# Dividing softmax probabilities inside the turning matmul, and one table set for Exp and Ln

## The reference, cut to what matters

```python
# first block: window attention (with a sink logit in the denominator)
p = jax.nn.softmax(logits, axis=-1);  o = einsum(p_win, v_i) + einsum(p_ctx, v_ctx)
# second block, NSA: three branches, each with its own gate
p = jnp.where(mask, jnp.exp(s - m), 0.0);  p = p / jnp.maximum(jnp.sum(p, -1), 1e-30)
o = gb[..., 0:1] * o_c + gb[..., 1:2] * o_s + gb[..., 2:3] * o_w
# second block, stick-breaking, 8 heads
log_rem = jnp.where(mask, jax.nn.log_sigmoid(-z), 0.0)
suffix = lax.cumsum(log_rem, axis=3, reverse=True) - log_rem
a = jnp.where(mask, jnp.exp(jax.nn.log_sigmoid(z) + suffix), 0.0)
# second block, memory cross attention, 4 heads
p = jax.nn.softmax(s, axis=-1)
```

## Time and profile before

| | us |
|---|---|
| median of 3 runs | 2379.2 (2374.57 to 2381.82) |
| the profiled execution | 2376.95 |
| its span | 2374.9 |
| TensorE busy | 2217.8 (93%) |
| VectorE busy | 1099.2 (46%) |
| ScalarE busy | 774.9 (33%) |

### The profile page before, as it was taken

How to read it: one execution, slowest core, us unless ns; L and a number is a source line. 1 busy time by engine, 2 the same in 40 slices (tenths; PEclk the granted TensorE clock), 3 DMA queues, 4 the chain that set the end, 5 groups by cost and what they waited for, 6 DMA issues and landing times.

```text
span 2374.9 us, 25076 instructions
## 1 busy us (share of the span) xinstructions
PE 2217.8 (93%) x10572; PEld 1763.5 (74%) x10572; DVE 1099.2 (46%) x1550; ACT 774.9 (33%) x1149; POOL 87.5 (4%) x84
## 2 busy tenths in 40 slices
PE   6997889999994999999999999899988898999999
PEld 4665678888873888888888888777755576888887
DVE  3637755555528433333534333453474346443421
ACT  4314432222223322222322222323455735222211
POOL 0000000000001000000111100100000001111100
PEclk9999999999996999999999999899887998999999
DMA  7521146555530232323223223223100021323232
GB/s 261 188 88 59 58 133 197 184 195 167 192 103 18 90 106 89 102 98 96 93 92 98 95 98 100 68 90 114 39 1 1 0 72 36 107 89 106 85 98 84
DMA packets 190784, 236.59 MB, mean 100 GB/s; under 512 B 4096, under 2 KB 175392, under 8 KB 190544
## 3 DMA queue, kind: packets, MB, share of 16 engines
q1 hardware_dynamic: 189696, 230.42, 30.1%
q0 software_dynamic: 976, 4.57, 0.6%
HBM read 231.96 MB, written 2.10 MB: 99 GB/s over the span
## 4 chain that ended last, share of the span: by engine, by line
PE 83%; DVE 8%; ACT 6%; issue 2%; DMA 0%; POOL 0%; SPq 0%; DVEq 0%; ACTq 0%; POOLq 0%
PE ps L402 24%; PE ps L403 24%; PE ps L404 24%; ACT pr L611 2%; PE ps L998 1%; PE ps L848 1%; PE ps L468 1%; PE ps L649 1%; DVE pr L636 1%; PE ps L1979 1%; PE ps L582 1%; PE ps L684 1%; DVE wl L351 1%; PE ps L381 1%; DVE sa L1397 1%
## 5 line engine op out<-in xcount | busy, mean ns | idle before, releaser
L402 PE MATMUL ps<-xh,wh 128*128 128x512 f32 x1800 | 714.8, 397 | 48.5 <-DVE xl L694 26.5
L403 PE MATMUL ps<-xl,wh 128*128 128x512 f32 x1800 | 708.1, 393 | 0.0
L404 PE MATMUL ps<-xh,wl 128*128 128x512 f32 x1800 | 707.3, 393 | 0.0
L351 DVE TENSOR_TENSOR wl<-raw,wh 128x2048 fp32r<-128x2048 f32 (+1 forms) x170 | 379.0, 2230 | 493.8 <-ACT wh L339 493.8
L402 PEld LDWEIGHTS ps<-xh,wh 128*128 128x128 f32 x1800 | 341.9, 190 | 128.6 <-issue 25.8
L339 ACT CAST wh<-raw 128x2048 fp32r<-128x2048 f32 (+1 forms) x170 | 314.5, 1850 | 340.7 <-PE ps L404 263.1
L404 PEld LDWEIGHTS ps<-xh,wl 128*128 128x128 f32 x1800 | 341.7, 190 | 73.1
L403 PEld LDWEIGHTS ps<-xl,wh 128*128 128x128 f32 x1800 | 342.1, 190 | 72.0 <-issue 1.2
L402 PE MATMUL ps<-hh,wh 128*128 128x512 f32 x704 | 274.1, 389 | 0.0
L404 PE MATMUL ps<-hh,wl 128*128 128x512 f32 x704 | 273.9, 389 | 0.0
L403 PE MATMUL ps<-hl,wh 128*128 128x512 f32 x704 | 273.9, 389 | 0.0
(11 more groups left out here) (331 smaller groups left out, 1892.4 us busy)
## 6 DMA issues: line engine op xcount, KB each, us to landing
raw<-in_ffn_w SPq DMA_DIRECT2D x52, 1024.0 KB, 5.4
raw<-in_ada_w SPq DMA_DIRECT2D x42, 1024.0 KB, 5.2
raw<-in_ffn_wg SPq DMA_DIRECT2D x22, 1024.0 KB, 5.4
raw<-in_ffn_wu SPq DMA_DIRECT2D x22, 1024.0 KB, 5.3
raw<-in_ffn_w SPq DMA_DIRECT2D x16, 896.0 KB, 4.6
raw<-in_ffn_wd SPq DMA_DIRECT2D x16, 896.0 KB, 4.7
raw<-in_w_in SPq DMA_DIRECT2D x10, 1024.0 KB, 5.2
raw<-in_ffn_wd SPq DMA_DIRECT2D x8, 1024.0 KB, 5.0
```

Source lines behind the costliest of these rows:

```text
L351: e.tensor_tensor(wl[s][:, 0:n], r[:, 0:n], wh[s][:, 0:n].bitcast(F32), ALU.subtract).then_inc(*WLO.up(i))
L402: e.matmul(dst, ah, bh, start=start, stop=False)
L403: e.matmul(dst, ah, bl, start=False, stop=False)
L404: return e.matmul(dst, al, bh, start=False, stop=stop)
```

## The change

`dve_scale` no longer writes the probabilities. It writes, for each head of the job, a 128x128 diagonal matrix that holds the reciprocals, into `tmp[job parity]`, with one tensor_tensor of the identity (repeated over heads) and the column (repeated over the row). `pe_turn` waits once for it, and uses an ordinary f32 matmul of the undivided probabilities by that diagonal in the place of the transpose by the identity. In the loop of ScalarE, ahead of the first stick-breaking head, a set of tables is loaded by name that holds both Exp and Ln.

```diff
-            for g in range(nh):
-                p = prs[J.name][:, J.par, g, 0:J.width]
-                e.tensor_scalar(p, p, rs[:, g:g + 1], None, ALU.mult).then_inc(*VS.up((J.name, "scaled", J.n, g)))
+            eye = ident.unsqueeze(1).broadcast_to([P, nh, P])
+            e.tensor_tensor(diagonal(J), eye, rs.unsqueeze(2).broadcast_to([P, nh, P]), ALU.mult).then_inc(
+                *VS.up((J.name, "diagonal", J.n)))
+
+        def diagonal(J):
+
+            return tmp[J.par][:, 0:J.heads * P].rearrange("p (g q) -> p g q", q=P)
 
         def pe_turn(e, J, banks=(4, 5, 7)):
-            first = True
+
+            e.wait_ge(*VS[J.name, "diagonal", J.n])
...
                     for g in range(J.heads):
-                        if first:
-                            e.wait_ge(*VS[J.name, "scaled", J.n, g])
                         o = (b * J.heads + g) * P
-                        m = e.transpose(bank[0:w, o:o + P], prs[J.name][:, J.par, g, col:col + w], ident)
-                    first = False
+                        m = e.matmul(bank[0:w, o:o + P], prs[J.name][:, J.par, g, col:col + w], diagonal(J)[:, g],
+                                     start=True, stop=True, skip_group_check=True)
...
                 elif s < NN + 8:
+                    if s == NN:
+                        e.preload_act_table_set("natural_log_exp_and_others")
                     act_stick_logs(e, s - NN)
```

## The result

The changed kernel takes 2355.9 us (median of 4 runs, 2353.6 to 2360.0) against 2379.9 (4 runs of before, 2374.6 to 2381.8). The ratio is 0.9909, with a 95% interval of 0.989 to 0.9928. So it is 24 us faster by the medians, and 23.3 us by the two profiled executions (2376.95 and 2353.65).

What follows compares the result with a forecast made beforehand. Chains round three engines, TensorE close behind, bound the attention stages. First attention -1.5, NSA -1, stick-breaking -11, clock -5, memory 0 make -18.5 from 2376.95: 2358.5, given as 2360 since the median is 2.25 higher; own range 2354 to 2366, outer 2345 to 2374.

Steps and rivals of the forecast that it cites:

- Table loads: Stick-breaking heads: 16 loads become one ahead of them; -11 us including 1.7 for longer turning; 1.24 us gained a steady head.
- The larger figure for a table switch: Stick-breaking heads: the Trainium skill's about 2.66 us a switch, drain included, 42.6 us in all; set aside for 1.28 a load.
- Turning and dividing: Three attentions: VectorE's shorter division is paid back by longer TensorE turns; first attention -1.5 us, NSA -1, memory 0.
- The clock: Stick-breaking stage: half of the 10 us lost at the low clock comes back as TensorE's waits shorten, -5 us.
- rival A: NSA and stick-breaking: every slow stretch goes as TensorE works almost without pause; -31.5 us, 2348; chance 0.14.
- B: Rival: only the loads pay, slow stretches stay or move; -10.5 us, 2369; chance 0.15.
- C: Rival: longer turning is exposed in narrow NSA jobs and at 1.2 GHz; about +10.5 us, 2390; chance 0.08.
- D: Rival: loads are still placed between Exp and Ln in the stick-breaking heads; 2378, no change; chance 0.05.

Runs made afterwards that it cites:

- the two kernels with fewer sums: Changed kernel and kernel before, each without the three matmuls a head that add the sums of later blocks: 2346.6 and 2380.3 us, one execution each.
- the tables alone: Kernel before with only the named table set added, transposes and divisions as before: 2361.2 us, ratio 0.993.
- the one with matmuls: Kernel before with the named table set, and turning by an ordinary matmul with the identity, divisions still on VectorE: 2358.4 us, ratio 0.9919.
- The two halves: Changed kernel without the named table set: 2375.1 us, ratio 0.9988; kernel before with only that set added: 2361.2 us, ratio 0.993.

## Why the prediction was right

The forecast was 2360 us, faster; measured were 2355.9. By its steps:

- **Table loads.** Right in mechanism; the size can't be read apart from the clock. One load is left, ahead of the first head, where ScalarE still waits 0.99 us for the scores behind it. The steady head was said to be 8.67 us with TensorE late next; it is 8.61, and the two kernels with fewer sums show that it is TensorE. My -11 us holds 1.7 for the longer turning, so the loads alone were forecast at -12.7 us, and the tables alone gave -16.0; but there the low clock of the stage also fell from 27.3 to 13.7 us. The larger figure for a table switch was rightly set aside: in the earlier trace rows a load ends at 1865.88 and the next begins at 1867.27, and the Ln of 1.36 us fills those 1.39, so no drain lies between:

```profile
1865.89 1.36 ACT L1996 ACTIVATE C2S<-C2S,cst 128x1280 f32<-128x1280 f32 x1
```

- **Turning and dividing.** The diagonals take 692 and 425 ns (0.68 and 0.42 taken). A turn costs more than the 0.2125 us that I took: I divided the time up to the next product's start in the earlier trace rows, where the last instruction starts 0.03 us ahead of it. The way I used for the transposes gives (1.95 - 0.27) / 15 = 0.112 an instruction, 0.224 a turn. That is the term behind the widest round, 18.3 us where I had 17.6 at full clock: its 36 turns took 8.46 us, with the start and end of each group, where I had 7.65, and all its other work 9.84 where I had 9.9. What made up for it was the clock in block 2. The outcome, VectorE's gain paid back to TensorE, held: 1.4 us in the NSA jobs (1 forecast), 0 in memory, and 0.2 in the first attention (1.5 forecast), less than the low stretches move that stage from one kernel to the next. The agreement in the NSA jobs is partly luck: by block it is +2.0, -0.3, -2.6 and -0.4 us, where I had the gain in block 3 and the others about even.
- **The clock.** The term that was too small. I counted half of the stick-breaking stage's 10 us; the stage had no low stretch at all. With -11 for the loads and -10 for the clock the stage would be -21, measured -19.8; how the 19.8 divide between the two no run shows. The low stretches of the later NSA jobs went too, as in rival A, but the 9 us that A put on them did not come back whole: block 2 lost 2.6 us and block 3 0.4, for at the full clock TensorE with the longer turning was the bound (no wait in the rows above).
- **The rivals.** A was half right, for the reason it gave (work without pause) and not for the rule cited beside it: the Trainium skill, "TensorE: Matmul & The Clock Gate", section "Part 4: PE-mode transpose", says that a transpose does not count as busy in the same way. The kernel with every f32 transpose twice had the clock of the one with matmuls, so here they count. B did not come: the slow stretches went, and even the tables without the turning gave -16.6 us, more than B's -10.5. C did not come as a whole, since at full clock the waits covered most of the longer turning; but the slow block 0, 2.0 us longer than before and for the most part at 1.2 GHz, is what its mechanism says of the low clock. D is ruled out by the one load.

The two halves do not add up by themselves: -2.7 and -16.6 us by the medians of their runs make -19, against -24 (the first is not told from nothing, so the medians alone would not carry this). The stick-breaking stage shows where: -0.2 and -16.0 alone, -19.8 together. Of these kernels only those with both, a longer turning before the stage and no loads in it, have the full clock through it.

## What to carry to other kernels

When a stall goes, look up the next engine's own round before counting the gain: 20.5 us of loads were worth 16 with what the clock gave back, and 1.3 us a steady head, not 2.6. In a chain that goes round several engines, moving work from VectorE to TensorE can pay through TensorE's clock, even where the moved work costs as much as it saves. Here it paid only once the loads were gone; alone it gave nothing that could be measured. Doubling the transposes for nothing shows how much of the gain is the clock. A small difference in a stage is not an effect before the same code has been profiled more than once: the same NSA code took 110.65 us in two executions and 112.1 in two others. Name a table set that holds both functions wherever two of them alternate.

## What the runs showed of the hardware

I had not expected that useless work could do as much as the change to the turning. With the tables named, issuing each of 368 transposes twice gave 2357.0 us, against 2361.2 with each once. The intervals of the two ratios overlap, but each of the four runs with doubled transposes is faster than each of the four without, and the granted clock in the later NSA jobs rose from 0.84 to 0.98. The opposite goes the same way, in one execution: taking 1.3 us of TensorE's work from each head of the kernel before left a head at the high level at 9.91 us, and brought the granted clock of these heads from 1.00 to 0.82.
